# Scattering an expert's output beside three gate steps of the next expert instead of four

## What is computed

```python
def moe_swiglu(x, w_router, b_router, we_gate, we_up, we_down):
    logits = (x @ w_router).astype(jnp.float32) + b_router.astype(jnp.float32)
    top_v, top_i = lax.top_k(logits, TOP_K)
    top_w = jax.nn.softmax(top_v, axis=-1)
    gates = jnp.sum(jax.nn.one_hot(top_i, N_EXPERTS, dtype=jnp.float32) * top_w[..., None], axis=-2)
    out = jnp.zeros(x.shape, jnp.float32)
    for e in range(N_EXPERTS):
        out = out + gates[..., e:e + 1] * swiglu(x, we_gate[e], we_up[e], we_down[e]).astype(jnp.float32)
    return out.astype(x.dtype)
```

## Time and profile before

| | |
|---|---|
| three runs | 1022.16, 1023.37, 1029.24 us; median 1023.37 |
| the profiled execution | 1020.04 us, of which the span of instructions is 1018.2 |
| granted clock, mean over the span | 0.967 |
| busy | PE 949.0, DVE 683.6, ACT 509.9, POOL 326.0 us |
| bytes read from HBM | 197.27 MB |

### The profile page before, as it was taken

One profiled execution on the slowest core, in us unless ns is written; L12 is line 12 of the kernel. 1 busy time (PEld: TensorE's weight loads), 2 busy tenths in 40 slices (PEclk: granted clock), 3 DMA queues, 4 the chain that ended last, 5 costly groups with the idle time before them and its releaser, 6 DMA issues.

```text
span 1018.2 us, 15036 instructions
## 1 busy us (share of the span) xinstructions
PE 949.0 (93%) x5514; PEld 791.6 (78%) x5514; DVE 683.6 (67%) x996; ACT 509.9 (50%) x645; POOL 326.0 (32%) x259
## 2 busy tenths in 40 slices
PE   5999797998999997999798999998999999999996
PEld 3576676998999996476587787887888788878774
DVE  7599446455343508696454386979788887878884
ACT  3641324453334402641432276768676856777662
POOL 7995002110455400960020025040414142332311
PEclk9998998999999998998998699999999999999998
DMA  9400830645654217301900298999898988898971
GB/s 275 147 1 3 296 104 23 216 151 154 166 160 150 89 42 211 106 3 51 372 1 1 91 348 287 312 319 324 286 304 290 374 277 309 287 376 277 383 229 47
DMA packets 95419, 199.64 MB, mean 196 GB/s; under 512 B 34178, under 2 KB 55906, under 8 KB 95236
## 3 DMA queue, kind: packets, MB, share of 16 engines
q1 hardware_dynamic: 94564, 197.88, 57.8%
q10 hardware_dynamic: 576, 0.59, 0.2%
q0 software_dynamic: 224, 0.43, 0.1%
HBM read 197.27 MB, written 1.61 MB: 195 GB/s over the span
## 4 chain that ended last, share of the span: by engine, by line
PE 85%; DVE 6%; DMA 4%; ACT 3%; issue 2%; DVEq 0%; SPq 0%; ACTq 0%
PE ps L1233 7%; PE ps L1232 7%; PE ps L1235 7%; PE ps L986 7%; PE ps L987 7%; PE ps L988 7%; PE ps L1148 5%; PE ps L1007 4%; PE ps L1303 4%; PE ps L999 4%; PE ps L1304 3%; PE ps L1307 3%; PE ps L1039 3%; DMA wraw_u<-in_moe_w_gate 3%; PE ps L1139 2%
## 5 line engine op out<-in xcount | busy, mean ns | idle before, releaser
L756 ACT ACTIVATE wrnd_g<-wraw_g 128x1376 fp32r<-128x1376 f32 (+2 forms) x96 | 115.4, 1214 | 64.5 <-DMA wraw_g<-in_moe_w_down 30.6
L623 POOL TENSOR_TENSOR wrnd_g<-wraw_g,wrnd_g 128x1024 fp32r<-128x1024 f32 (+2 forms) x16 | 48.7, 3046 | 298.5 <-ACT wrnd_g L756 298.5
L1351 DVE TENSOR_TENSOR wrnd_u<-wraw_u,wrnd_u 128x1376 fp32r<-128x1376 f32 (+1 forms) x80 | 138.5, 1760 | 3.9 <-ACT wrnd_u L756 3.5
L1351 DVE TENSOR_TENSOR wrnd_g<-wraw_g,wrnd_g 128x1376 fp32r<-128x1376 f32 (+1 forms) x80 | 118.4, 1492 | 20.1 <-ACT wrnd_g L756 19.8
L756 ACT ACTIVATE wrnd_u<-wraw_u 128x1376 fp32r<-128x1376 f32 (+1 forms) x96 | 115.6, 1257 | 12.7 <-DMA wraw_u<-in_moe_w_gate 8.5
L1351 DVE TENSOR_TENSOR xb<-xb,ps 128x288 f32<-128x288 f32 x96 | 39.1, 446 | 64.7 <-PE ps L1148 41.4
L623 POOL TENSOR_TENSOR wrnd_u<-wraw_u,wrnd_u 128x1376 fp32r<-128x1376 f32 (+1 forms) x16 | 53.3, 3329 | 87.7 <-ACT wrnd_u L756 87.7
L986 PE MATMUL ps<-Md,split_u 128*128 128x288 f32 (+2 forms) x240 | 71.4, 297 | 2.7 <-DVE rs L1351 2.7
L988 PE MATMUL ps<-Md,split_u 128*128 128x288 f32 (+2 forms) x240 | 70.9, 295 | 0.0
L986 PE MATMUL ps<-Md,split_d 128*128 128x288 f32 (+2 forms) x224 | 66.0, 295 | 0.8 <-DVE xb L1351 0.8
L988 PE MATMUL ps<-Md,split_d 128*128 128x288 f32 (+2 forms) x224 | 65.6, 293 | 0.0
(11 more groups left out here) (337 smaller groups left out, 2623.3 us busy)
## 6 DMA issues: line engine op xcount, KB each, us to landing
wraw_u<-in_moe_w_gate SPq DMA_DIRECT2D x39, 688.0 KB, 6.4
wraw_g<-in_moe_w_up SPq DMA_DIRECT2D x32, 688.0 KB, 7.7
wraw_g<-in_moe_w_down SPq DMA_DIRECT2D x39, 512.0 KB, 4.6
wraw_u<-in_moe_w_down SPq DMA_DIRECT2D x33, 512.0 KB, 4.3
wraw_u<-in_moe_w_up SPq DMA_DIRECT2D x24, 688.0 KB, 5.7
wraw_g<-in_moe_w_gate SPq DMA_DIRECT2D x18, 688.0 KB, 5.9
raw<-in_ffn_w_gate SPq DMA_DIRECT2D x20, 512.0 KB, 4.2
raw<-in_ffn_w_up SPq DMA_DIRECT2D x20, 512.0 KB, 4.2
```

Source lines behind the costliest of these rows:

```text
L623: pool.tensor_tensor(lo[0:r, 0:w], raw_half(n)[0:r, 0:w], hi[0:r, 0:w].bitcast(F32), ALU.subtract).then_inc(w_lo_pool, 1)
L756: act.activation(halves(n)[0][0:r, 0:w], raw_half(n)[0:r, 0:w], ACT.Copy).then_inc(w_hi, 1)
L1351: return dve.tensor_tensor(o, a, b, op)
```

## The change

The eight blocks are scattered behind three gate steps instead of four: blocks 0 and 1 behind gate 5, blocks 2 to 4 behind gate 6, blocks 5 to 7 behind gate 7. The banks go round in threes: blocks 5, 6 and 7 use banks 5, 6 and 7, where they used 6, 7 and 6. Each of blocks 5 to 7 now waits for the add of the block three before it instead of two (block 5 waited for the add of block 3, now of block 2). Up 0 of the next expert waits for six adds instead of three, since block 5 is in bank 5. DVE's adds follow: blocks 0 and 1 in its step for gate 6, 2 to 4 in that for gate 7, 5 to 7 at the end. Nothing is added or removed: the numbers of matmuls, adds, highs and lows are the same. Lines behind the edit move down by 2 to 4.

```diff
--- before.py
+++ after.py
@@ -89,7 +89,9 @@
 POOL_STEPS = (12, 15, 18, 21, 25)
 POOL_LEAD = (2, 5)
 ACT_AHEAD, LOW_AHEAD = 5, 4
-SCATTER_BANK = (3, 4, 5, 6, 7, 6, 7, 6)
+
+SCATTER_AT = {5: (0, 1), 6: (2, 3, 4), 7: (5, 6, 7)}
+SCATTER_BANK = (3, 4, 5, 6, 7, 5, 6, 7)
 END_BANK = (3, 4, 5, 0, 1, 2, 6, 7)
 assert len(STEPS) == PER and 2 * PER % NSLOT == 0 and NSLOT > LEAD
 
@@ -1248,7 +1250,7 @@
                 elif k == 3:
                     pe.wait_ge(yel_ready, each(i, a, 2, 2))
                 elif k >= 5 and not end:
-                    pe.wait_ge(xadd, each(i, a, 8, X_MOE + k - 1))
+                    pe.wait_ge(xadd, each(i, a, 8, X_MOE + k - 2))
                 f = slice(k * P, (k + 1) * P)
                 b = (END_BANK if end else SCATTER_BANK)[k]
                 pe.matmul(bank(b), ye_h[:, f], sgt, start=True, stop=False)
@@ -1271,7 +1273,7 @@
 
                 for q, (kind, k) in enumerate(steps):
                     if q == 0:
-                        pe.wait_ge(xadd, each(i, a, 8, X_MOE - 8 + 3))
+                        pe.wait_ge(xadd, each(i, a, 8, X_MOE - 8 + 6))
                         if a == 0:
                             pe.wait_ge(hgbl_ready, i + 1)
                     if kind == "up":
@@ -1322,8 +1324,8 @@
                                 pe.wait_ge(hgl_ready, i * 4 + 5)
                             r = (4, 5, 8, 9).index(k)
                             gather(r, (4, 3, 5, 4)[r])
-                    if kind == "gate" and k >= 4:
-                        for m in (2 * k - 8, 2 * k - 7):
+                    if kind == "gate":
+                        for m in SCATTER_AT.get(k, ()):
                             scatter(m, i, a, gathers)
                 if last:
                     for m in range(KT):
@@ -1774,15 +1776,15 @@
                            ALU.subtract).then_inc(hgl_ready, 1)
                     if q == d0 + FT:
                         output_dve(i, a)
-                    if steps[q][0] == "gate" and steps[q][1] >= 5:
-                        for m in (2 * steps[q][1] - 10, 2 * steps[q][1] - 9):
+                    if steps[q][0] == "gate":
+                        for m in SCATTER_AT.get(steps[q][1] - 1, ()):
                             add_scattered(m, i, a)
                     n = n0 + q + LOW_AHEAD
                     if not moe_by_pool(n) and (not final or n < ends + len(LAST_STEPS)):
                         moe_low(n, i, ends)
                 if last:
                     output_dve(i, a)
-                for m in range(0 if last else 6, KT):
+                for m in range(KT) if last else SCATTER_AT[KT - 1]:
                     add_scattered(m, i, a, last)
 
             with dve.Fori(0, more) as i:
```

## The result

Nine runs of the changed kernel gave 1029.83 to 1040.32 us, median 1034.84; nine of the one before 1012.55 to 1030.12, median 1023.37. The ratio is 1.0151 with a 95% interval of 1.0112 to 1.019: slower by 1.5%, some 15 us where 8.7 were forecast, and just above the range (1.0151 x 1023.37 = 1038.8). With all nine on each side the ratio is 1.0130, or 13.3 us, and the time 1036.7, inside the range. The profiled execution took 1036.17 us, its span is 1034.4.

The account below looks back on a forecast made before the run. PE was taken to bound the kernel, with DVE's list setting its waits. Later up 0 starts, 7.0 us, plus one clock fall, 1.7, made 8.7 more; against the runs' median, 3.3 above the profiled execution, 1032 us, range 1026 to 1038.

Parts of the forecast that it names:

- What bounds the kernel: Whole kernel: PE, busy 949.0 us of the span of 1018.2, so the change is worth what it does to PE's waits.
- The rule: Boundaries between experts: new start of up 0 = old start of the last pair of adds + 0.23 us.
- The forecast sum: Later starts of up 0 at four waiting boundaries and three without waits: together 7.0 us more, before the clock.
- The waits: PE at the boundaries: output wait goes, 1.7 to 2.7 us ahead of `scatter(5)` at four, new wait ahead of up 0 at seven.
- The clock: Waiting boundaries: PE's granted clock falls once, at the first one, for half of 3.4 us, 1.7 us more.
- the one at 244.88: Trace of before: PE waited 2.66 us for DVE, then the clock was 0.50 for 3.4 us; basis of the clock term.
- rival 2: Clock falls at three or four waiting boundaries, or lasts twice as long at some: 12.1 to 20.6 us more; chance 0.16.
- Rival 3: DMAs take back the delay of boundaries without waits within the next expert: 3.9 us more, 1027.3 us; chance 0.13.
- rival 1: Clock never falls at the waiting boundaries: 7.0 us more, 1030.4 us; chance 0.22.
- Rival 4: Adds keep up and all waits go at the four waiting boundaries: some 12 us faster, 1011 us; chance 0.05.

Follow-up runs that it names:

- e8_wait8: The changed kernel with up 0 waiting for all eight adds instead of six; 1.0198 times the kernel before.

## Why the prediction was wrong in size

*What bounds the kernel, and that DVE's place in its own list tells when up 0 starts:* right. The rule, old start of the last pair of adds + 0.23, amounts to 11.26 behind the output; measured 11.23 to 11.24 at the three boundaries without late output and at one of the others, 11.33 at the three behind a loop's branch. The forecast sum was 7.0; the starts in the trace give 6.9, and the runs 6.8 at equal clock.

*The waits:* the first one went, as forecast (1.9 us left, 1.6 of them at the end). The one ahead of `scatter(5)` was forecast at 1.7 to 2.7, measured 2.42, 1.67, 0.93 and 1.79. That ahead of up 0 was forecast as 0.9 and 1.7; the list has up to 1.5, since modelled ends lie late.

*The clock:* here the sum failed. The step said that only the boundary whose wait is as long as the one at 244.88 loses the clock, once, for half of 3.4 us, and counted none of the other three. Measured: in the two profiles of the changed kernel six of eight waiting boundaries lost it, for 3.4 or 6.8 us each, 34 us in all or 17 in an execution (14 and 20; the second profile is of the slowest run of its six). Over the runs the half-clock time is 16.4 us more. At 0.41 a us that is 6.7 us where 1.7 stood. The sum 6.8 + 6.7 = 13.5 us is the difference of the mean times of the 15 and 67 runs by the way the line is fitted, and so no test of it; the tests are the 6.9 us of the starts, and the 6.5 us that the filled waits gave back.

Two things were wrong in it. I took the one row that had lost the clock, 2.66 us of idling, as the length that it takes, and counted shorter idles as nothing. Three of the four longest falls came behind a first idle of 2.42, 2.30 or 2.41, the fourth behind one of 1.79, and all four before the second idle had begun; the other two came with up 0, behind both idles (0.93 and 1.51, 1.79 and 1.41). And a fall was taken as 3.4 us, when those four lasted 6.8. The rows of before, where waits of 1.7 and 1.28 lying 5 us apart kept the clock, showed one execution that kept it, and no length that always does: in the changed kernel 1.67 and 1.51 kept it and 0.93 and 1.51 did not. What decides between two such boundaries stays open, and so does how much the second idle adds.

The Trainium skill ("TensorE: Matmul & The Clock Gate", "HAM oscillation — how this bites in real kernels") would by its rule have had no fall at all at these boundaries, since no single idle here is as long as the gap it names. The trace disagrees: 2.42 us of idling ahead of 700.96 were enough.

*The rivals:* rival 2 is what happened, at its lower end (12.1 more was its floor). Rival 3 is refuted by the intervals between boundaries and by e8_wait8, rival 1 by the profiles. Rival 4 was right that less than 10.4 us behind the output for up 0 pays in a waiting boundary, and wrong that a single low less would do: that gained 0.3 to 0.4 us at each of the four and lost 0.37 at each of the other three, and the kernel came out even. It took two.

## What to carry to other kernels

When a step is moved from before to behind an instruction of another engine's list, count that engine's list from the last thing that starts it, at every place where the other side waits; the sum is exact to a tenth of a us when the list has no gap. Before moving work on the engine that waits, ask whether reordering the engine that is waited for gets the same for nothing: two lows moved on DVE turned 1.5% slower into 0.7% faster. And price idle time on TensorE with the clock: here 1 us at half clock cost 0.4 us, and new idles of 0.9 to 2.4 us, two to a boundary, lost the clock at six boundaries of eight, not only at those as long as the one seen to lose it before.

## What the runs showed of the hardware

- The clock fell to 0.50 in six of eight boundaries that held an idle of 0.9 to 2.4 us ahead of `scatter(5)`, about 0.8 us of matmuls and 1.1 to 1.5 us of idling ahead of up 0, and in none of eight when the same waits were filled to no more than 0.91 us of idling at a time. The falls that began ahead of the second idle lasted 6.8 us, the others 3.4.
- The same wait does not always end the same way. Ahead of the last scatter of the program PE idles for 1.64 us in all twelve profiles. In eight of them (the changed kernel's 1018.7 is one) the clock fell between its end and 1.3 us behind, in four (before, both filled ones, adds one low sooner) it did not.
- Matmuls whose result nobody reads, issued into a free bank, are a cheap cure: 18 of them at each of four boundaries gained 6.5 us, and delayed up 0 by less than 0.1.
- From a scatter's matmul to DVE's add and back to PE's next matmul, with all engines free, takes longer than the four matmuls of two more blocks (0.53 us): up 0 started 0.48 us behind the last of them instead of 0.13.
- Half-clock time outside the changed code differs from run to run of one kernel by tens of us (clock 0.948 to 0.972, or 57 to 108 us at half clock, in the 67 runs of the kernel before). It goes with most of the scatter of their times: 4.1 us of standard deviation, and 1.5 around the fitted line.
